# Axial attention in a two-layer encoder: products with the values issued in batches behind every fourth head

## The chip, the cores and the metric

The kernel runs on one core of a Trainium2 chip. The metric is the device time of one execution in microseconds (us). Engines: PE does matmuls and transposes, DVE element-wise work and reductions, ACT activations and copies, SP issues most of the transfers; each runs its own queue in order, and they meet in semaphores.

## The reference

Two groups of tokens, a prompt of 512 and a sample of 1024, go through the same two layers (1024 channels). The second layer's mixer is axial attention; its core is plain softmax attention within each group, in blocks of 128 queries, with 16 heads of 64 channels and 4 key/value heads:

```python
def attend(qi):
    s = jnp.einsum('bqkgd,bskd->bkgqs', qi, k).astype(jnp.float32) * scale
    p = jax.nn.softmax(s, axis=-1).astype(v.dtype)
    return jnp.einsum('bkgqs,bskd->bqkgd', p, v)
```

Everything else (projections, rotary, the first layer's convolution and window attention, a mixture of experts behind each mixer, layer norms) is the same before and after.

## The kernel before

The function axial_attention (from L1790) is one stage of the program. It runs over the prompt part (4 tiles of 128 queries against 512 keys), then the sample part (8 tiles against 1024 keys). A tile has two sides, each with a **set** of 8 heads; so the prompt part has 8 sets, the sample part 16.

For each head n of a set the chain over the engines is:

- PE, `qk` (L1884): scores of 128 queries against all keys into one of two score buffers, s_ps. Two heads share one buffer in turn, so qk waits until the exponential of the head two before has read it. The call stands two heads ahead (AHEAD = 2).
- DVE, `top` (L1938): the row maximum of s_ps. ACT, `exps` (L1981): exponential and row sum into p. DVE, `invert` (L1942): the reciprocal of the sum. ACT, `norm` (L1986): p times the reciprocal.
- PE, `turn` (L1892): transposes p block by block into t_ps (one buffer); it waits for norm of this head and for the copy of the head before. DVE, `copy` (L1949): t_ps to pT.

A set's pT is used one set later: PE, `pv` (L1899), multiplies it with the values, one key block k at a call, accumulating in o_ps. ACT, `out` (L1990), copies o_ps to cat, once in a set, behind `norm` of head 2 of a later set (behind the last set of a part, at the end).

The order on each engine is written out by hand and does not depend on time. PE, for each head n: qk(n+2), turn(n), and pv(set before, n) while n is below the number of key blocks, which is 4 in the prompt part and 8 in the sample part. DVE: top(n), copy(n-2), invert(n). ACT: exps(n), norm(n), and out behind n = 2. The first set of a part has no set before it and so no products; behind a part's last set the products of all key blocks of that set follow in a row. Middle tiles run in a hardware loop.

Of the kernel before, what the change touches and what calls it, by code (L numbers as in the profile page):

```python
# [14 lines left out]
P = 128  # L15
# [1773 lines left out]
def axial_attention(c, m, keys, values, cat, early):  # L1789
    nc = c.nc  # L1790
    SET = AX_H // 2
    SHARE = SET // 2
    AHEAD = 2
    NB = 4
    with c.stage():
        ident = c.sb("ident", [P, P])
        q = c.sb("q", [P, 2, SET * P], F32R)
        p = c.sb("p", [P, NB, SEQ[1]])
        pT = c.sb("pT", [P, 2, SEQ[1] // P, SET, P])
        col = c.sb("col", [P, NB, 4])  # L1800
        s_ps, t_ps, o_ps = [c.ps("s_ps0", SEQ[1]), c.ps("s_ps1", SEQ[1])], c.ps("t_ps", SEQ[1]), [c.ps("o_ps0", HALF), c.ps("o_ps1", HALF)]
# [12 lines left out]
        def schedule(eng, g, run):  # L1814


            first, tiles = GROUP_FIRST[g], GROUP_TILES[g]
            run(first, 0, 0, False)
            run(first, 1, 1, False)
            with eng.Fori(0, tiles - 2) as i:  # L1820
                run(i + (first + 1), 0, 2, False)
                run(i + (first + 1), 1, 2, False)
            run(first + tiles - 1, 0, 2, False)
            run(first + tiles - 1, 1, 2, True)

        def set_before(tile, side):
            return (tile, 0) if side == 1 else (tile - 1, 1)

        def number(tile, side, n=0):

            return tile * AX_H + (side * SET + n)

        with c.block() as block:

            @block.sync
            def _(sp):
                sp.dma_start(ident[:], m["ident"]).then_inc(loaded, 16)
                def load(t):
                    for side in range(2):

                        sp.wait_ge(scores, number(t, side, SET))
                        sp.dma_start(q[:, side, :].bitcast(F32), m["qT_parts"][bass.ds(t * P, P), side * SET * P:(side + 1) * SET * P]).then_inc(q_in[side], 16)

                load(0)
                for to in range(2):
                    sp.dma_start(group(to, 1, 1).bitcast(F32), group(1, 1, 0).bitcast(F32)).then_inc(spread_in, 16)
                with sp.Fori(1, GROUP_TILES[0]) as t:
                    load(t)
                sp.wait_ge(spread_in, 32)
                sp.dma_start(group(1, 1, 0).bitcast(F32), group(0, 1, 0).bitcast(F32)).then_inc(spread_in, 16)  # L1850
                with sp.Fori(GROUP_TILES[0], GROUP_TILES[0] + 2) as t:
                    load(t)

                sp.wait_ge(scores, number(GROUP_TILES[0], 0, 2 * SET))
                for k in range(len(early)):
                    for side, rows in enumerate(out_weight_rows(m, 1, k)):
                        sp.dma_start(early[k][DH * side:DH * (side + 1)], rows.rearrange("p (j n) -> p j n", j=2)).then_inc(weights_in, 16)
                with sp.Fori(GROUP_TILES[0] + 2, TILES) as t:
                    load(t)
                sp.wait_ge(weights_in, 32 * len(early))  # L1860

            @block.tensor
            def _(pe):
                pe.sem_inc(scores, 2 * SET)
                pe.sem_inc(pT_done, NB)
                pe.sem_inc(pv_done, 2)
                pe.wait_ge(loaded, 16)
                for g in range(len(SEQ)):
                    nk, first = SEQ[g], GROUP_FIRST[g]
                    if g == 0:  # L1870
                        pe.wait_ge(keys_ready, 1)
                    else:
                        pe.wait_ge(spread_in, 48)

                    def qk(tile, side, n):
                        if n >= SET:
                            tile, side, n = (tile, 1, n - SET) if side == 0 else (tile + 1, 0, n - SET)
                        if n == 0:
                            pe.wait_ge(q_in[side], tile * 16 + 16)
                        pe.wait_ge(expd, number(tile, side, n + 1))  # L1880
                        for b in range(nk // HALF):
                            at = first * P + b * HALF
                            for part in range(2):
                                last = nc.tensor.matmul(s_ps[n % 2][:, b * HALF:(b + 1) * HALF], q[:, side, n * P:(n + 1) * P],  # L1884
                                                        keys[:, part * AX_KV + 2 * side + n // SHARE, at:at + HALF], start=(part == 0), stop=(part == 1))
                        last.then_inc(scores, 1)

                    def turn(tile, side, n):
                        pe.wait_ge(p_ready, number(tile, side, n + 1))
                        pe.wait_ge(pT_ready, number(tile, side, n + 1))  # L1890
                        for k in range(nk // P):
                            last = nc.tensor.transpose(t_ps[:, k * P:(k + 1) * P], p[:, n % NB, k * P:(k + 1) * P], ident[:])  # L1892
                        last.then_inc(pT_done, 1)

                    def pv(tile, side, k):
                        if k == 0:
                            pe.wait_ge(o_out, tile * 2 + side + 1)
                        for kv in range(2):
                            last = nc.tensor.matmul(o_ps[side][DH * kv:DH * (kv + 1), :], values[:, first + k, (2 * side + kv) * DH:(2 * side + kv + 1) * DH],  # L1899
                                                    pT[:, side, k, SHARE * kv:SHARE * (kv + 1), :].rearrange("p h n -> p (h n)"),  # L1900
                                                    start=(k == 0), stop=(k == nk // P - 1))
                        if k == nk // P - 1:
                            last.then_inc(pv_done, 1)

                    def run(tile, side, before, at_last):
                        for n in range(SET):
                            if not (at_last and n + AHEAD >= SET):
                                qk(tile, side, n + AHEAD)
                            turn(tile, side, n)
                            if before and n < nk // P:  # L1910

                                pv(*set_before(tile, side), n)

                    for n in range(AHEAD):
                        qk(first, 0, n)
                    schedule(pe, g, run)
                    pe.wait_ge(pT_ready, number(first + GROUP_TILES[g], 0, 1))
                    for k in range(nk // P):
                        pv(first + GROUP_TILES[g] - 1, 1, k)

            @block.vector
            def _(v):
# [10 lines left out]
                for g in range(len(SEQ)):  # L1933
                    nk, first = SEQ[g], GROUP_FIRST[g]

                    def top(tile, side, n):
                        v.wait_ge(scores, number(tile, side, n + 1 + 2 * SET))
                        nc.vector.tensor_reduce(col[:, n % NB, 0:1], s_ps[n % 2][:, 0:nk], AX.X, ALU.max, negate=True).then_inc(top_ready, 1)  # L1938

                    def invert(tile, side, n):  # L1940
                        v.wait_ge(expd, number(tile, side, n + 3))
                        nc.vector.reciprocal(col[:, n % NB, 2:3], col[:, n % NB, 1:2]).then_inc(inverse, 1)  # L1942

# [134 lines left out]
def trunk(nc, m):  # L2078
# [6 lines left out]
    with c.stage():  # L2085
# [23 lines left out]
        with c.stage():  # L2109
            assert next_address(nc) == at_keys  # L2110
            under_keys = nc.alloc_sbuf_tensor_at("under_keys", [P, 2 * AX_KV, TOK], F32, offset=at_keys)
            keys, values = c.sb("keys", [P, 2 * AX_KV, TOK], F32R), c.sb("values", [P, TILES, AX_KVD])
            project_axial(c, m, keys, values, at_keys, under_picks, soon)
            cat = c.sb("cat", [P, KD, TOK])
            early = [early_weight(under_keys, k) for k in range(3)]
            axial_attention(c, m, keys, values, cat, early)

            project_out(c, m, 1, early, m["x2"], cat, picks, keys[:].rearrange("p k n -> p (k n)"))
# [49 lines left out]
```

## Time and profile before

| what | value |
|---|---|
| median of three runs | 3653.29 us (3652.67 to 3654.38) |
| the profiled execution's own time | 3651.85 us |
| its span | 3650.1 us |
| axial attention in it, first score product to last product with values | 1929.7 to 2449.0 us |
| PE, DVE, ACT busy over the whole span | 91%, 70%, 56% |
| PE's granted clock, mean over the span | 0.954 |

The page's shares are means over all stages; experts, projections and the first layer hold most of the span. What the change touches lies within the 519 us of axial attention: 128 us of prompt part and 393 us of sample part. So the views that count are cut to that stretch: busy time by window, and the instructions in order of time with the idle time before each and what ended it. A PE row with a count (x8) is a group of merged matmuls; its start is exact, its end is modelled, so distances between PE groups are read from start to start. In traces each matmul of the products appears as two rows, so one key block (two matmuls) is x4.

### The profile page before, as it was taken

How to read it: one execution, taken by the hardware profiler on the slowest of the kernel's cores; microseconds unless marked ns; L12 is line 12 of the kernel's file. 1: busy time of each engine (PE TensorE's matmuls, PEld its weight loads, DVE VectorE, ACT ScalarE, POOL GpSimd, SP SyncE). 2: the span in 40 equal slices, each digit the busy share in tenths (PEclk: the TensorE clock that was granted, in tenths of full speed). 3: DMA queues.
4: the chain of work that ended last, by engine and by line, in shares of the span. 5: the costliest groups of instructions: out<-in, count | busy, mean ns of one | idle time of the engine just before them, and what ended most of it. 6: DMA issues, size and time to landing. Idle time of an engine off the chain costs nothing. (4 is left out here: it accounts for less than half of the span.)

```text
span 3650.1 us, 51757 instructions
## 1 busy us (share of the span) xinstructions
PE 3305.2 (91%) x18872; PEld 2770.0 (76%) x18872; DVE 2544.8 (70%) x4025; ACT 2031.4 (56%) x2823; POOL 391.0 (11%) x309
## 2 busy tenths in 40 slices
PE   8995779599999999978987899999869999999993
PEld 7883468499999999966873456658769999999992
DVE  4988945776676766747766788875666676666765
ACT  3117942266666666643437788762246666666664
POOL 0000011111111111102210000001111111111102
PEclk9998989699999999998988999999879999999996
DMA  3001223577777777753322110013277787777864
GB/s 125 32 33 42 67 78 117 168 256 251 255 241 246 259 247 248 240 166 108 108 77 76 35 41 23 23 38 125 98 258 253 234 259 247 259 246 237 258 218 158
DMA packets 361095, 588.84 MB, mean 161 GB/s; under 512 B 17680, under 2 KB 284048, under 8 KB 359440
## 3 DMA queue, kind: packets, MB, share of 16 engines
q1 hardware_dynamic: 339728, 511.75, 41.7%
q0 software_dynamic: 14336, 50.34, 6.1%
q10 hardware_dynamic: 6912, 25.17, 1.7%
q8 instruction: 73, 1.20, 0.1%
q14 instruction: 46, 0.38, 0.0%
HBM read 505.42 MB, written 78.64 MB: 160 GB/s over the span
## 5 line engine op out<-in xcount | busy, mean ns | idle before, releaser
L1256 PE MATMUL h_ps<-xT,high 128*128 128x384 f32 x3584 | 1068.5, 360 | 2.7 <-DVE xT L1378 2.7
L1374 DVE TENSOR_TENSOR low<-raw,high 128x2048 fp32r<-128x2048 f32 x384 | 876.8, 2284 | 155.8 <-ACT high L1318 148.4
L1257 PE MATMUL h_ps<-xT,low 128*128 128x192 f32 x3584 | 906.7, 253 | 0.0
L1318 ACT ACTIVATE high<-raw 128x2048 fp32r<-128x2048 f32 x384 | 734.3, 1913 | 283.4 <-PE yp_ps L1289 176.2
L1257 PEld LDWEIGHTS h_ps<-xT,low 128*128 128x128 f32 x3584 | 686.4, 192 | 1.3
L1256 PEld LDWEIGHTS h_ps<-xT,high 128*128 128x128 f32 x3584 | 677.0, 189 | 5.0 <-issue 3.5
L1439 DVE TENSOR_TENSOR gate_up<-h_ps,cross 128x384 f32<-128x384 f32 x256 | 142.7, 558 | 298.8 <-ACT cross L1337 298.8
L1337 ACT ACTIVATE cross<-h_ps 128x384 f32<-128x384 f32 x256 | 125.6, 491 | 264.9 <-PE h_ps L1260 264.8
L200 DVE SCALAR_TENSOR_TENSOR cat<-glu,taps,cat 128x272 f32<-128x272 f32 (+33 forms) x480 | 256.7, 603 | 0.0
L1938 DVE TENSOR_REDUCE col<-s_ps 128x1 f32<-128x1024 f32 (+1 forms) x192 | 200.4, 1044 | 62.2 <-PE s_ps L1884 61.8
L1981 ACT ACTIVATE p<-s_ps,col 128x1024 f32<-128x1024 f32 (+1 forms) x192 | 186.5, 971 | 57.8 <-DVE col L1938 57.8
L1986 ACT ACTIVATE p<-p,col 128x1024 f32<-128x1024 f32 (+1 forms) x192 | 193.5, 1008 | 44.3 <-DVE col L1942 44.3
L1884 PEld LDWEIGHTS s_ps<-keys,q 128*128 128x128 f32 x640 | 106.4, 190 | 146.0 <-issue 130.9
L1884 PE MATMUL s_ps<-keys,q 128*128 128x512 f32 x640 | 199.6, 426 | 14.5 <-DMA q<-rows_qT_parts 12.0
L1280 PE MATMUL y_ps<-low,hT 128*128 128x512 f32 x512 | 204.1, 399 | 0.0
L1279 PE MATMUL y_ps<-high,hT 128*128 128x512 f32 x512 | 204.0, 398 | 0.0
L1285 PE MATMUL yp_ps<-high,hT 128*128 128x512 f32 x512 | 201.9, 394 | 0.0
L1289 PE MATMUL yp_ps<-low,hT 128*64 128x512 f32 x512 | 201.7, 394 | 0.0
L1949 DVE COPY pT<-t_ps 128x1024 f32<-128x1024 f32 (+1 forms) x192 | 198.9, 1036 | 3.4 <-PE t_ps L1892 3.4
L1278 PE MATMUL y_ps<-high,hT 128*128 128x512 f32 x512 | 201.2, 393 | 0.0
L1892 PEld LDWEIGHTS t_ps<-ident,p 128*128 128x128 f32 x1280 | 148.0, 141 | 65.6 <-ACT p L1986 26.6
L1892 PE MATMUL t_ps<-ident,p 128*128 128x128 f32 x1280 | 172.7, 274 | 26.3 <-DVE pT L1949 26.1
(254 smaller groups left out, 5943.3 us busy)
## 6 DMA issues: line engine op xcount, KB each, us to landing
raw<-moe_w_gate SPq DMA_DIRECT2D x128, 1024.0 KB, 5.3
raw<-moe_w_up SPq DMA_DIRECT2D x128, 1024.0 KB, 7.7
raw<-moe_w_down SPq DMA_DIRECT2D x128, 1024.0 KB, 7.0
rows_x<-x ACTq DMA_DIRECT2D x24, 512.0 KB, 2.6
rows_acc<-ax ACTq DMA_DIRECT2D x24, 512.0 KB, 2.7
r<-rows_acc SPq DMA_DIRECT2D x24, 512.0 KB, 5.9
rows_qT_parts<-q_turned SPq DMA_DIRECT2D x12, 1024.0 KB, 4.0
q<-rows_qT_parts SPq DMA_DIRECT2D x24, 512.0 KB, 3.8
```

The costliest lines, as they stand in the source:

```text
L200: return nc.vector.scalar_tensor_tensor(conv[:, one, lo:hi], glu[:, one, lo + step:hi + step], weight, conv[:, one, lo:hi], ALU.mult, ALU.add)
L1256: nc.tensor.matmul(ps, wh[:, n, k, :], xT[:, u, place(k), :, :].rearrange("p s n -> p (s n)"), start=(k == 0), stop=False)
L1257: nc.tensor.matmul(ps[:, 0:SLOTS], wl[:, n, k, :], xT[:, u, place(k), 0, :], start=False, stop=False)
L1278: nc.tensor.matmul(y_ps[:, cols], hT[:, f, 0:SC], wh[:, j, cols], start=first, stop=False)
L1279: nc.tensor.matmul(y_ps[:, cols], hT[:, f, SC + 2 * PC:2 * SLOTS], wh[:, j, cols], start=False, stop=False)
L1280: nc.tensor.matmul(y_ps[:, cols], hT[:, f, 0:SC], wl[:, j, cols], start=False, stop=end)
L1285: return nc.tensor.matmul(yp_ps[:, cols], hT[:, f, SC:SC + 2 * PC], wh[:, j, cols], start=first, stop=end)
L1289: return nc.tensor.matmul(yp_ps[0:PC, cols], hT[:, f, SC:SLOTS], wl[:, j, cols], start=False, stop=False)
L1318: nc.scalar.activation(split_view(high, at), piece_view(at), ACT.Copy).then_inc(high_ready, 1)
L1374: nc.vector.tensor_tensor(split_view(low, at), piece_view(at), split_view(high, at).bitcast(F32), ALU.subtract).then_inc(low_ready, 1)
L1884: last = nc.tensor.matmul(s_ps[n % 2][:, b * HALF:(b + 1) * HALF], q[:, side, n * P:(n + 1) * P], keys[:, part * AX_KV + 2 * side + n // S ...
L1892: last = nc.tensor.transpose(t_ps[:, k * P:(k + 1) * P], p[:, n % NB, k * P:(k + 1) * P], ident[:])
```

## The change

On PE alone, the call of pv moves. Where each of a set's first heads had one key block of products behind its transposes, now the heads 3 and 7 have several: in the sample part four blocks each, in the prompt part two each. The other heads have none. The order of the blocks, the buffers, the semaphores and the other engines' programs stay.

```diff
     NB = 4
+    TOGETHER = 4
...
                             turn(tile, side, n)
-                            if before and n < nk // P:
-
-                                pv(*set_before(tile, side), n)
+                            if before and n % TOGETHER == TOGETHER - 1:
+                                steps = nk // P * TOGETHER // SET
+                                for k in range(n // TOGETHER * steps, n // TOGETHER * steps + steps):
+                                    pv(*set_before(tile, side), k)
```

PE's queue in the sample part, second set, heads 0 to 3, before (s_ps are scores, t_ps transposes, o_ps products with the values; the numbers tell buffers apart):

```order
L1884 MATMUL s_ps_297<-keys,q 128x512 x4
L1892 MATMUL t_ps<-ident,p 128x128 x8
L1899 MATMUL o_ps_300<-pT,values 64x512 x2
L1884 MATMUL s_ps_298<-keys,q 128x512 x4
L1892 MATMUL t_ps<-ident,p 128x128 x8
L1899 MATMUL o_ps_300<-pT,values 64x512 x2
L1884 MATMUL s_ps_297<-keys,q 128x512 x4
L1892 MATMUL t_ps<-ident,p 128x128 x8
L1899 MATMUL o_ps_300<-pT,values 64x512 x2
L1884 MATMUL s_ps_298<-keys,q 128x512 x4
L1892 MATMUL t_ps<-ident,p 128x128 x8
L1899 MATMUL o_ps_300<-pT,values 64x512 x2
```

The same heads, and the first product of the next, in PE's queue of the changed kernel, whose lines are one further on:

```order
L1885 MATMUL s_ps_297<-keys,q 128x512 x4
L1893 MATMUL t_ps<-ident,p 128x128 x8
L1885 MATMUL s_ps_298<-keys,q 128x512 x4
L1893 MATMUL t_ps<-ident,p 128x128 x8
L1885 MATMUL s_ps_297<-keys,q 128x512 x4
L1893 MATMUL t_ps<-ident,p 128x128 x8
L1885 MATMUL s_ps_298<-keys,q 128x512 x4
L1893 MATMUL t_ps<-ident,p 128x128 x8
L1900 MATMUL o_ps_300<-pT,values 64x512 x8
L1885 MATMUL s_ps_297<-keys,q 128x512 x4
```

Four calls of one block have become one row of four blocks (eight matmuls), which stands between the transposes of head 3 and the scores of head 6.

PE's queue in the prompt part, second set, heads 4 to 7, in the changed kernel; before, these rows held s_ps and t_ps alone:

```order
L1885 MATMUL s_ps_297<-keys,q 128x512 x2
L1893 MATMUL t_ps<-ident,p 128x128 x4
L1885 MATMUL s_ps_298<-keys,q 128x512 x2
L1893 MATMUL t_ps<-ident,p 128x128 x4
L1885 MATMUL s_ps_297<-keys,q 128x512 x2
L1893 MATMUL t_ps<-ident,p 128x128 x4
L1885 MATMUL s_ps_298<-keys,q 128x512 x2
L1893 MATMUL t_ps<-ident,p 128x128 x4
L1900 MATMUL o_ps_300<-pT,values 64x512 x4
```

Two blocks that stood behind heads 2 and 3 stand behind head 7 now. DVE's queue in the sample part, which is the same before and after but for the line numbers (here before):

```order
L1938 TENSOR_REDUCE col<-s_ps_297 128x1
L1949 COPY pT<-t_ps 128x8x128
L1942 RECIPROCAL col<-col 128x1
L1938 TENSOR_REDUCE col<-s_ps_298 128x1
L1949 COPY pT<-t_ps 128x8x128
L1942 RECIPROCAL col<-col 128x1
```

Nothing moved there: maximum n, copy n-2, reciprocal n, and then the maximum of the next head.

## Rows read from the trace of the kernel before

**Rows 1.** The page's head: span and instructions of the profiled execution.
```profile
span 3650.1 us, 51757 instructions
```
**Rows 2.** Busy us (instructions) of PE, PEld, DVE, ACT, POOL by window, clock, DMA.
```profile
2056.00:2080.00 24.00, 17.71 (x98) 12.63 (x96) 19.21 (x24) 20.10 (x26) 0.00 (x0) 1.00 0.07 23
2150.00:2250.00 100.00, 100.00 (x533) 59.70 (x532) 84.03 (x101) 79.88 (x105) 0.00 (x0) 1.00 0.06 21
```
**Rows 3.** Order of time (start, duration, instruction): sample part, heads with products.
```profile
2089.91 1.08 PE L1899 MATMUL o_ps<-pT,values 128*64 128x512 f32 x4
...
2090.92 1.19 PE L1884 MATMUL s_ps<-keys,q 128*128 128x512 f32 x4
...
2091.95 1.03 PE L1892 MATMUL t_ps<-ident,p 128*128 128x128 f32 x8
2092.15 1.22 DVE L1938 TENSOR_REDUCE col<-s_ps 128x1 f32<-128x1024 f32 x1 [0.34 <-PE s_ps L1884]
...
2092.92 1.08 PE L1899 MATMUL o_ps<-pT,values 128*64 128x512 f32 x4
```
**Rows 4.** Order of time: sample part, first set, heads without products.
```profile
2065.09 1.20 DVE L1938 TENSOR_REDUCE col<-s_ps 128x1 f32<-128x1024 f32 x1
...
2066.21 1.21 DVE L1949 COPY pT<-t_ps 128x1024 f32<-128x1024 f32 x1
2066.32 1.12 ACT L1981 ACTIVATE p<-s_ps,col 128x1024 f32<-128x1024 f32 x1
...
2067.56 0.17 DVE L1942 RECIPROCAL col<-col 128x1 f32<-128x1 f32 x1
2067.57 1.06 PE L1892 MATMUL t_ps<-ident,p 128*128 128x128 f32 x8 [0.57 <-DVE pT L1949]
2067.64 1.21 DVE L1938 TENSOR_REDUCE col<-s_ps 128x1 f32<-128x1024 f32 x1
2067.76 1.15 ACT L1986 ACTIVATE p<-p,col 128x1024 f32<-128x1024 f32 x1 [0.23 <-DVE col L1942]
...
2068.39 1.17 PE L1884 MATMUL s_ps<-keys,q 128*128 128x512 f32 x4
2068.88 1.12 ACT L1981 ACTIVATE p<-s_ps,col 128x1024 f32<-128x1024 f32 x1
```
**Rows 5.** Order of time: end of the prompt part, four blocks of products in a row.
```profile
2050.96 5.27 PE L1899 MATMUL o_ps<-pT,values 128*64 128x512 f32 x16 [0.78 <-DVE pT L1949]
2051.87 0.24 PEld L1899 LDWEIGHTS o_ps<-pT,values 128*64 128x64 f32 x2 [0.61 <-issue]
2052.73 0.24 PEld L1899 LDWEIGHTS o_ps<-pT,values 128*64 128x64 f32 x2 [0.62 <-issue]
```
**Rows 6.** Order of time: ACT's evacuation of the products, sample part.
```profile
2110.92 0.58 ACT L1990 ACTIVATE cat<-o_ps 128x512 f32 x1
```
**Rows 7.** Order of time: sample part, first transposes of set 2, final eight blocks.
```profile
2082.91 1.06 PE L1892 MATMUL t_ps<-ident,p 128*128 128x128 f32 x8 [0.56 <-DVE pT L1949]
...
2441.89 7.09 PE L1899 MATMUL o_ps<-pT,values 128*64 128x512 f32 x32 [0.31 <-DVE pT L1949]
```
**Rows 8.** Order of time: prompt part, from heads without to heads with products.
```profile
1974.59 0.69 DVE L1938 TENSOR_REDUCE col<-s_ps 128x1 f32<-128x512 f32 x1
...
1976.02 0.63 PE L1892 MATMUL t_ps<-ident,p 128*128 128x128 f32 x4 [0.53 <-DVE pT L1949]
...
1976.22 0.69 DVE L1938 TENSOR_REDUCE col<-s_ps 128x1 f32<-128x512 f32 x1
...
1976.58 1.08 PE L1899 MATMUL o_ps<-pT,values 128*64 128x512 f32 x4
...
1977.59 0.73 PE L1884 MATMUL s_ps<-keys,q 128*128 128x512 f32 x2
...
1978.35 0.69 DVE L1938 TENSOR_REDUCE col<-s_ps 128x1 f32<-128x512 f32 x1 [0.43 <-PE s_ps L1884]
...
1978.68 1.08 PE L1899 MATMUL o_ps<-pT,values 128*64 128x512 f32 x4
```
**Rows 9.** Order of time: prompt part, first transposes of set 2.
```profile
1945.95 0.63 PE L1892 MATMUL t_ps<-ident,p 128*128 128x128 f32 x4 [0.54 <-DVE pT L1949]
```

## The prediction, made before the changed kernel was run

> **What bounds the kernel now.** I read the page first, then the windows of the stage, then the order of time in it, because the change touches one stage only and the page's shares mix all of them. The profiled execution spans 3650.1 us [rows 1]; its own time is 3651.85 us, 1.75 us more, and the median of three runs is 3653.29 us. So a difference read from the trace is added to 3653.29 at the end.
>
> The windows [rows 2] hold the point of departure. In the sample part, where products with the values run (the second row), PE is busy 100.00 of 100 us, DVE 84 and ACT 80. In the first set of the sample part, which has no such products (the first row), PE is busy 17.71 of 24 us and DVE and ACT 19 to 20, with little idle between their instructions. The granted clock is 1.00 in both. So there are two regimes in one stage, and the order of time shows what limits each.
>
> With the products [rows 3]: PE goes o_ps, s_ps, t_ps, o_ps without a gap, at 2089.91, 2090.92, 2091.95 and 2092.92. A head costs 1.01 + 1.03 + 0.97 = 3.01 us of PE, and the next maximum on DVE has waited 0.34 us for PE. PE is the bound.
>
> Without them [rows 4]: maximum to maximum is 2067.64 - 2065.09 = 2.55 us. The loop goes from the maximum (2065.09) to the exponential (2066.32) to the reciprocal (2067.56) to the next maximum (2067.64). PE needs only 1.03 (s_ps to t_ps, [rows 3]) + 0.82 (t_ps 2067.57 to s_ps 2068.39, [rows 4]) = 1.85 us for such a head. DVE and ACT are the bound, and ACT has no slack either: the scaling at 2067.76 is followed by the next exponential at 2068.88, as it ends.
>
> So a head's floor is 2.55 us on DVE/ACT, and the products put 3.01 - 1.85 = 1.16 us of PE into each head, spread evenly. The whole question is what happens if that work comes in lumps.
>
> **What the change does, part by part.** The same matmuls are issued (on PE in another order; on DVE and ACT every instruction stands where it stood), so no work is removed or added; no DMA and no queue of SP or POOL is moved.
>
> *Gain on PE.* Products that follow one another are cheaper than one block between other matmuls. At the end of the prompt part four blocks run in a row: the weight loads that start a new block stand at 2051.87 and 2052.73, 0.86 us apart [rows 5]; between other matmuls a block takes 1.01 us to the next s_ps [rows 3]. A lump of four costs 3 x 0.86 + 1.01 = 3.59 us in place of 4.04. Per four heads PE's work goes from 4 x 3.01 = 12.04 us to 4 x 1.85 + (0.97 + 3.59 - 0.82) = 11.14 us. If PE stayed the bound this would be the result: 0.9 us less per four heads.
>
> *Loss by coupling.* PE stands in order, and behind the lump on PE stands the score product of head n+3 (s_ps). DVE's queue is fixed: maximum n, copy n-2, reciprocal n, maximum n+1. When the lump starts behind the transposes of head 3, scores exist for heads up to 5 and no more. In the regime that DVE sets, the transposes of head 3 start 0.15 us after the copy of head 2 has ended (2066.21 + 1.21 = 2067.42 to 2067.57 [rows 4]). From that copy's end DVE has left: reciprocal 4, maximum 5, copy 3, reciprocal 5, together about 0.17 + 1.21 + 1.21 + 0.17 = 2.8 us, that is up to about 1.7 us after the lump's start. Then maximum 6 waits for s_ps of head 6, which PE starts only 3.59 us after the lump's start and which is there 1.23 us later (2090.92 to 2092.15 [rows 3]), at 4.82 us. DVE and behind it ACT stand for about 3 us in each lump. PE then waits in turn: heads 4 to 7 come from DVE and ACT again at their floor.
>
> *One round of four heads, sample part*, from the start of one lump to the start of the next: lump to s_ps 3.59; s_ps to maximum 6, 1.23; two heads at DVE/ACT's floor, maximum 6 to 8, 5.10; maximum 8 to the transposes of head 7 behind the copy of head 6, 2067.57 - 2065.09 = 2.48 [rows 4]; transposes to lump 0.97 [rows 3]. Sum 13.37 us, against 12.04 before: +1.33. The transposes of head 4 (1.03 after s_ps) and the scores of 7 and 8 come before DVE asks for them, so nothing else is late.
>
> *The evacuation.* ACT's copy of o_ps to cat takes 0.58 us once in a set, behind head 2's scaling [rows 6]. Before, ACT had waiting time there. Afterwards it falls into the heads just behind a lump, at ACT's floor, where it delays the next exponential, hence the reciprocal, hence the next maximum. I count it in full, 0.58 in every second round, and keep 0 as the other end.
>
> *Sum, sample part.* The second set's first transposes start at 2082.91 and its fourth would start three heads at 2.55 later, at 2090.56 (before: three heads at 3.01, so 1.4 us are won here). From there to the eighth head of the last set are 14 sets of 8 and 4 heads, 29 rounds, of which 14 hold an evacuation: 29 x 13.37 + 14 x 0.58 = 395.8 us. That puts the last set's eighth transposes at 2486.4; 0.97 + 4 x 0.86 = 4.4 us later the final eight blocks start, at 2490.8. Before they start at 2441.89 [rows 7]. Loss 48.9 us. The final eight blocks are the same in both.
>
> *Prompt part.* DVE's floor is 1.63 us (maximum 1974.59 to 1976.22 [rows 8]); the products come in heads 0 to 3 alone, 2.10 us a head (1976.58 to 1978.68, o_ps to o_ps). After the change two lumps of two blocks. A round: 0.86 + 1.01 to s_ps, 0.76 to the maximum (1977.59 to 1978.35), two heads 3.26, maximum to the next head's transposes 1.43 (1974.59 to 1976.02), 0.56 to the lump: 7.88 us, and 0.58 in every second one. First transposes of the second set 1945.95 [rows 9], the fourth 4.89 later at 1950.84; 13 rounds with 6 evacuations, 13 x 7.88 + 6 x 0.58 = 105.9, to 2056.8; 0.56 + 2 x 0.86 later, 2059.0, the final four blocks, before at 2050.96 [rows 5]. Loss 8.1 us.
>
> Together 48.9 + 8.1 = 57 us: 3653.3 + 57 = **3710 us**. Later stages begin later and are not touched.
>
> *Unknown sizes.* If the evacuation is hidden, 14 x 0.58 + 6 x 0.58 = 11.6 us less, 3698. If a block in a lump costs 1.01 and not 0.86, 29 x 0.45 + 13 x 0.15 = 15 us more, 3725. I take the rows' middle course, evacuation in full (nearest row: ACT back to back in rows 4) and 0.86 (nearest row: the same four blocks in a row).
>
> **The rivals.**
> *The lump is hidden and only the PE gain is left (faster).* This needs DVE and ACT to have enough queued at a lump's start to work until s_ps returns, 4.82 us of it where I count about 1.7. It breaks even when the standing time of 3 us shrinks to about 1.4. Then a round costs PE's 11.14 us, 0.9 less than now, 29 times, and in the prompt part DVE's floor, 4 x 1.63 = 6.5 in place of 2 x (2.10 + 1.63) = 7.5, 13 times: 26 + 13 = 39 us, 3614 us. For it: PE is busy 100% in the row where the products run, and blocks in a row are cheaper. Against it: two banks of scores, so only two heads ahead, and DVE's fixed order. 5%.
>
> The Trainium skill speaks for this rival: Perfetto Trace Analysis, Matmul Optimizations, says that the matmul engine scales its power with its use and that matmuls should therefore run back to back in batches. The trace gives that no room by way of the clock, since 1.00 is granted in both windows [rows 2]; by the rule with the cheaper blocks alone the time would be this rival's 3614 us, by the rows with the coupling 3710 us.
>
> *Partly hidden, gain and stall cancel.* A stall of about 1.4 us in a round; nothing in the rows sets it so. Within 0.2% (about what a measurement of this kernel can tell from no change), near 3653. 2%.
>
> *The lump is wholly in series.* If maximum 5 and copy 3 gain nothing beside the lump, a round is four heads at 2.55 and the lump's 3.74, 13.94 in place of 13.37: 29 x 0.57 = 17 us more, 3727, and with dearer blocks up to 3742. Against it: the scores of head 5 stand in PE's queue before the lump. 8%.
>
> **How the numbers follow.** The forecast, 3710 us with 3694 to 3728 about it, has 85%: 3698 and 3725 are its computed ends, and some 4 us are added for what rows of one execution leave open. The range is that one; what is left out is the two small cases on the fast side and the upper part of the serial one. Faster by over 0.2% 5%, within 2%, slower 93%.
>
> **What would show it.** In the profile after: rounds in the sample part of about 13.4 and 13.9 us, o_ps in rows of four blocks 3.6 us from the next s_ps; idle time of DVE before its maximum of about 3 us, twice in a set; PE waiting about 0.6 us for pT in the heads without products; PE near 83% (11.14 of 13.37) in windows where it had 100%; the stage longer by 57 us and the rest as before. Wrong would be: PE without gaps in the sample part (the first rival), no long waits of the maximum for s_ps, or a granted clock other than 1.00 there, since all durations are from rows at that clock.

## The result, and the profile after

The changed kernel takes 3715.19 us (median of four runs, 3712.45 to 3716.38) against 3653.81 us of the kernel before in the same comparison: 61.4 us more, a ratio of 1.0166 with a 95% interval of 1.0151 to 1.0181. The forecast was 3710 us, 57 us more, in a range of 3694 to 3728.

The page of the changed kernel begins like this (span, then busy time of each engine, its share and its instructions):

```profile
span 3714.6 us, 51757 instructions
PE 3295.9 (89%) x18872; PEld 2771.6 (75%) x18872; DVE 2538.8 (68%) x4025; ACT 2029.1 (55%) x2823; POOL 384.4 (10%) x309
```

The number of instructions is that of [rows 1], and PE's busy time is a little less (3305.2 us before): no work was added, so the time is waiting. Axial attention runs from its first score product to its last product with the values for 520.2 us before (its first score product starts at 1928.7 us, not at 1929.7) and 582.1 us after, 61.9 us more, so the difference lies there; the whole span is 64.5 us longer, of which 3.1 us had come before the stage began.

The window of the sample part after the change (us of PE, PEld, DVE, ACT, POOL; then granted clock and transfers), which answers to the second row of [rows 2]:

```profile
2103.00:2486.00 383.00, 322.48 (x1784) 199.77 (x1780) 275.00 (x335) 267.08 (x349) 0.00 (x0) 1.00 0.07 22
```

PE is busy 84% where it was busy 100%, DVE 72% where it was 84%. The clock is 1.00 as before. All engines are less busy: they wait for one another.

PE in order of time, one round of the sample part (start, duration, instruction, idle time before and what ended it), which answers to the PE rows of [rows 3]:

```profile
2197.81 1.07 PE L1893 MATMUL t_ps<-ident,p 128*128 128x128 f32 x8 [0.60 <-DVE pT L1951]
2198.80 3.65 PE L1900 MATMUL o_ps<-pT,values 128*64 128x512 f32 x16
2202.39 1.21 PE L1885 MATMUL s_ps<-keys,q 128*128 128x512 f32 x4
2203.43 1.04 PE L1893 MATMUL t_ps<-ident,p 128*128 128x128 f32 x8
2204.22 1.17 PE L1885 MATMUL s_ps<-keys,q 128*128 128x512 f32 x4
...
2212.68 3.65 PE L1900 MATMUL o_ps<-pT,values 128*64 128x512 f32 x16
```

There are four blocks in one lump, 3.59 us to the next scores, and 13.88 us from lump to lump. This is a round with an evacuation (ACT's copy of o_ps to cat); a round without one takes 13.50 us. DVE in the same stretch:

```profile
2199.04 1.22 DVE L1951 COPY pT<-t_ps 128x1024 f32<-128x1024 f32 x1
2200.39 0.17 DVE L1944 RECIPROCAL col<-col 128x1 f32<-128x1 f32 x1
2203.63 1.22 DVE L1940 TENSOR_REDUCE col<-s_ps 128x1 f32<-128x1024 f32 x1 [3.07 <-PE s_ps L1885]
2204.77 1.21 DVE L1951 COPY pT<-t_ps 128x1024 f32<-128x1024 f32 x1
```

DVE has finished its last reciprocal 1.76 us after the lump's start (2200.56) and stands until the scores are there, 4.83 us after it. The idle time before the maximum is 3.07 us, where [rows 3] had 0.34. The totals of waiting over 300 us of the sample part (us in total, times, longest):

```profile
DVE col L1940 <- PE s_ps L1885: 64.4, 21, 3.1
PE t_ps L1893 <- DVE pT L1951: 48.4, 66, 1.0
```

The waits go both ways. DVE waits once in a round, about 3.07 us; PE then waits in each of the other three heads, 0.73 us on average, for DVE's copy to free t_ps. Before, in the same stretch of time, DVE's waits were 34.2 us in 100 small ones, and PE's waits of this kind came to 1.1 us in all the sample part's heads with products but the last two (2080 to 2436 us).

### The profile page after: what moved, and what is told of

It is laid out like the page before. It is cut to its first block and busy times, and to the rows that moved or that the text cites. A ratio compares the mean times of both kernels' runs of the same rounds, so it can differ in the third digit from the quotient of the medians.

```text
span 3714.6 us, 51757 instructions
## 1 busy us (share of the span) xinstructions
PE 3295.9 (89%) x18872; PEld 2771.6 (75%) x18872; DVE 2538.8 (68%) x4025; ACT 2029.1 (55%) x2823; POOL 384.4 (10%) x309
## 5 line engine op out<-in xcount | busy, mean ns | idle before, releaser
L1184 POOL TENSOR_TENSOR still<-still 128x1 f32<-128x1 f32 x98 | 26.1, 268 | 1609.2 <-DVE work L1456 1297.3
```

## The experiments

The first theory is that of the prediction: a lump on PE holds back the scores and the transposes that DVE needs, DVE and ACT run dry, and PE then waits for them in turn. Its rivals: PE stays the bound and gains by cheaper blocks; the lump stands wholly in series; the two score buffers alone are the reason. In every run below only axial attention differs from one of the two kernels.

| run | us | ratio to before, 95% |
|---|---|---|
| e1, lumps in the sample part only | 3706.6 | 1.0146 (1.0129 to 1.0163) |
| e2, lumps in the prompt part only | 3661.6 | 1.0020 (1.0011 to 1.0030) |
| e3, lumps half as large | 3686.1 | 1.0086 (1.0069 to 1.0103) |
| e5, scores ahead of the lump | 3693.8 | 1.0105 (1.0088 to 1.0122) |
| e6, evacuation one head earlier | 3707.6 | 1.0149 (1.0134 to 1.0165) |
| e7, prompt part in half blocks | 3662.6 | 1.0024 (1.0014 to 1.0034) |
| e8, two transpose buffers, every second head | 3640.6 | 0.9966 (0.9952 to 0.9979) |
| e9, two transpose buffers alone | 3649.8 | 0.9990 (0.9980 to 0.9999) |
| e10, lumps with two transpose buffers | 3651.4 | 0.9997 (0.9988 to 1.0006) |

### e1 and e2: each part by itself

The condition at the call of pv is made to depend on the part g (0 the prompt, 1 the sample); e2 has `g == 0`:

```diff
+                            if g == 1:
+                                if before and n % TOGETHER == TOGETHER - 1:
+                                    steps = nk // P * TOGETHER // SET
+                                    for k in range(n // TOGETHER * steps, n // TOGETHER * steps + steps):
+                                        pv(*set_before(tile, side), k)
+                            elif before and n < nk // P:
+                                pv(*set_before(tile, side), n)
```

> Lumps of four blocks in the sample part only; the prompt part as in the kernel before. Theory (PE's lump holds back the next scores and transposes, DVE and ACT stand for about 3 us, every round goes from 12.04 to about 13.4 and 13.9 us): the sample part's whole loss, 49 us by the forecast's sum and about 54 by the changed kernel's trace, so 3703 to 3708 us; the prompt part's sets stay near 15.05 us. Rival (the parts act on each other, say by the granted clock or the transfers): less than 45 us or more than 60 us.

> Lumps of two blocks in the prompt part only; the sample part as in the kernel before. Theory: 8 us over the kernel before, 3662 us, with prompt rounds of 7.9 and 8.4 us in place of 7.5, and the sample part's sets at 24.05 us. Rival (in the prompt part DVE's floor alone counts, since PE has room): about 13 us faster than before, 3641 us.

Measured: 3706.6 us, 53 us more than before (3653.9), and 3661.6 us, 8 us more. Together 61 us, what the whole change costs. The sets of the part left alone are unchanged (3.00 to 3.01 us a head in the sample part of e2). The two parts add up and do not act on each other; the rivals of both are out.

### e3: lumps half as large

```diff
-    TOGETHER = 4
+    TOGETHER = 2
```

> Lumps of two blocks behind every second head in the sample part, one block behind every second head in the prompt part. Theory: a round of two heads in the sample part is lump to scores 0.86 + 1.01, scores to maximum 1.23, maximum to the next head's transposes 2.48, transposes to lump 0.97, together 6.55 us in place of 6.02; 59 rounds, 31 us; the evacuation falls into DVE's and ACT's standing time and costs nothing; the prompt part's round is 1.01 + 0.76 + 1.43 + 0.56 = 3.76 us, as much as two heads now on average. So about 3685 us, half the change's loss with half its lump. Rival one (PE stays the bound and gains by blocks in a row): 5.72 us a round, 17 us faster, 3637. Rival two (the lump is in series with DVE's floor): 7.1 us a round, 64 us slower, 3718.

Measured: 3686.1 us, 32 us more than before. In the sample part every round is 6.59 or 6.60 us (6.55 expected), in the prompt part 3.77 (3.76). DVE and PE in order of time, sample part of e3:

```profile
2193.06 1.94 PE L1900 MATMUL o_ps<-pT,values 128*64 128x512 f32 x8
2194.93 1.20 PE L1885 MATMUL s_ps<-keys,q 128*128 128x512 f32 x4
...
2196.16 1.23 DVE L1940 TENSOR_REDUCE col<-s_ps 128x1 f32<-128x1024 f32 x1 [0.98 <-PE s_ps L1885]
...
2198.67 1.06 PE L1893 MATMUL t_ps<-ident,p 128*128 128x128 f32 x8 [0.74 <-DVE pT L1951]
```

The lump is 1.87 us to the next scores instead of 3.59. The cheaper-blocks rival (3637) and the serial one (3718) are both out, on opposite sides. In the sample part, where all of this loss lies, it grows with the lump, but not in proportion: that part is 34 us longer than before with lumps of two blocks and 54 us with lumps of four. The prompt part of e3, with one block behind every second head, is 2 us shorter than before in the trace.

### e5: the scores ahead of the lump

```diff
-                            if not (at_last and n + AHEAD >= SET):
+                            early = n == TOGETHER if before else False
+                            early = early or (n == 0 and before == 2)
+                            if not early and not (at_last and n + AHEAD >= SET):
                                 qk(tile, side, n + AHEAD)
                             turn(tile, side, n)
+                            if before and n % TOGETHER == TOGETHER - 1 and not (at_last and n + AHEAD + 1 >= SET):
+                                qk(tile, side, n + AHEAD + 1)
```

> The changed kernel with one move on PE: the scores of head n+3 are issued ahead of the lump and not behind it, in both parts. The third score product finds its buffer free, since the exponential of the head two before is over by then. Theory (both products of PE that DVE needs, scores and transposes, stand behind the lump): the wait only moves from the maximum of head 6 to the copy of head 4, a round in the sample part falls from 13.4 to about 12.9 us and in the prompt part from 7.9 to 7.65: 14 and 3 us less than the changed kernel, 3698 us. Rival (the two score buffers alone are the reason): with the scores there in time the stall is gone and PE's 11.1 us a round remain, 3614 us. Rival (place of the scores is no matter): 3715 us.

Measured: 3693.8 us, 21 us less than the changed kernel and still 40 us more than before. The rounds of the sample part are 12.95 us, 13.22 to 13.25 where the hardware loop turns and 13.42 with an evacuation. DVE and PE in order of time:

```profile
2201.51 3.65 PE L1900 MATMUL o_ps<-pT,values 128*64 128x512 f32 x16
2202.17 0.16 DVE L1948 RECIPROCAL col<-col 128x1 f32<-128x1 f32 x1
2202.27 1.22 DVE L1944 TENSOR_REDUCE col<-s_ps 128x1 f32<-128x1024 f32 x1
2205.09 1.09 PE L1893 MATMUL t_ps<-ident,p 128*128 128x128 f32 x8
2206.22 1.22 DVE L1955 COPY pT<-t_ps 128x1024 f32<-128x1024 f32 x1 [2.73 <-PE t_ps L1893]
```

The maximum runs beside the lump now, and then DVE stands 2.73 us before the next copy, which waits for the transposes behind the lump. The wait has moved, as expected, so the score buffers are not the reason by themselves: DVE needs two products of PE for each head, and both stand behind the lump. The gain was 21 us and not 17: in the trace the sample part gave 15 us (14 expected) and the prompt part 6 (3 expected; its plain rounds are 7.43 us and not 7.65).

### e6: the evacuation one head earlier

```diff
-                            if n == AHEAD and before == 2:
+                            if n == 1 and before == 2:
```

> The changed kernel with ACT's evacuation of o_ps one head earlier, behind head 1's scaling and not head 2's. There ACT stands idle in the lump behind head 7. Theory: the evacuation then costs nothing; by the forecast's sum 20 x 0.58 = 11.6 us less than the changed kernel, by the rounds of its trace (13.88 with it, 13.50 without; 8.36 and 7.92 in the prompt part) 14 x 0.38 + 6 x 0.44 = 8 us less: 3704 to 3707 us. Rival (it was hidden already and the longer rounds come from elsewhere): 3715 us.

Measured: 3707.6 us, 7.6 us less than the changed kernel's 3715.2. ACT and DVE in order of time, sample part of e6:

```profile
2197.38 0.60 ACT L1992 ACTIVATE cat<-o_ps 128x512 f32 x1 [0.85 <-PE o_ps L1900]
2198.41 1.23 DVE L1940 TENSOR_REDUCE col<-s_ps 128x1 f32<-128x1024 f32 x1 [3.06 <-PE s_ps L1885]
2199.67 1.11 ACT L1983 ACTIVATE p<-s_ps,col 128x1024 f32<-128x1024 f32 x1 [1.69 <-DVE col L1940]
```

The copy of 0.60 us lies in time in which ACT waits anyway, and the rounds of 13.88 us are gone: three of four are 13.50 to 13.52, and the fourth, where the loop turns, 13.80 to 13.82. So the evacuation did cost something in the changed kernel, 0.37 us a set in the sample part and not 0.58.

### e7: the prompt part in half blocks

The change's opposite, on the kernel before: half a key block behind each head of the prompt part.

```diff
-                            if before and n < nk // P:
-
+                            if before and g == 0:
+                                pv(*set_before(tile, side), n // 2, (n % 2,))
+                            elif before:
                                 pv(*set_before(tile, side), n)
```

Here pv takes the list of its matmuls as an argument, and waits and signals only at the first and last of the set.

> The kernel before with the change's opposite in the prompt part: each of the 8 heads of a set has half a key block of products (one of its two matmuls), where heads 0 to 3 had one block each; the sample part as before. Theory (PE's work should be spread as evenly as DVE's floor allows): a head costs PE 0.53 + 0.58 + 0.57 = 1.68 us, near DVE's 1.63, so a set takes 13.4 us in place of 15.05: 7 sets, 11 us faster than before, 3643 us. Rival (two half blocks apart lose what runs side by side in one block, so that half a block costs as much as a whole one): 2.1 us a head, 16.8 a set, 12 us slower, 3666 us.

Measured: 3662.6 us, 9 us slower than before. The price that the theory put on half a block was wrong here, and the rival held (3666 by its sum). PE in order of time, prompt part of e7:

```profile
1955.35 1.07 PE L1899 MATMUL o_ps<-pT,values 128*64 128x512 f32 x2
1956.35 0.73 PE L1884 MATMUL s_ps<-keys,q 128*128 128x512 f32 x2
1956.92 0.60 PE L1892 MATMUL t_ps<-ident,p 128*128 128x128 f32 x4
1957.45 1.07 PE L1899 MATMUL o_ps<-pT,values 128*64 128x512 f32 x2
```

One matmul (x2 in the trace) takes 1.00 us to the next scores, and [rows 8] have 1.01 us for the two of a whole block (x4). The two write different halves of o_ps's partitions and run side by side: in the trace of the kernel before their rows start within 0.01 us of each other. Taken apart, each costs as much as both. Each head takes 2.10 us, all eight of a set.

### e8, e9 and e10: room for PE to run ahead

In the prompt part a head's transposes fill half of t_ps. With the two halves used in turn the transposes wait for the copy of the head two before. e9 has this alone:

```diff
-                        pe.wait_ge(pT_ready, number(tile, side, n + 1))
+                        pe.wait_ge(pT_ready, number(tile, side, n + 1 + g))
+                        at = 0 if g else (n % 2) * HALF
...
-                v.sem_inc(pT_ready, 1)
+                v.sem_inc(pT_ready, 2)
```

Transposes and copy use columns from `at` on. In e9 the first products of a set also wait for the last copy of that set, since the transposes no longer do. e10 has the two halves and the lumps of e2; e8 has the two halves and one block behind every second head, by this edit:

```diff
-                            if before and n < nk // P:
-
-                                pv(*set_before(tile, side), n)
+                            if before and (g or n % 2):
+                                pv(*set_before(tile, side), n if g else n // 2)
```

> The kernel before with two edits in the prompt part, nothing in the sample part: the transposes go to two halves of t_ps in turn, so that they wait for the copy of the head two before and not of the head before; and one block of products stands behind every second head, where it stood behind heads 0 to 3. Theory (PE's work must come evenly, and PE must be allowed to run ahead of DVE): two heads need 2 x 1.1 + 1.0 = 3.2 us of PE and 3.26 of DVE and ACT, so a set takes about 13.3 us in place of 15.05: 12 us faster than before, 3641 us. Rival (the transposes' one buffer was no matter): rounds of 3.77 us as with products behind every second head and one buffer, no change, 3654 us.

> The control for the run before: two halves of t_ps in the prompt part alone, the products where they were, behind heads 0 to 3. Theory: four heads in a row still need 2.1 us of PE each, and two score buffers let PE run ahead by part of a head only, so 0 to 1 us a set, 0 to 7 us faster, about 3650 us. Rival (the buffer does it all): 12 us faster, 3641 us.

> Lumps of two blocks in the prompt part only, as in the run with the prompt part alone, and two halves of t_ps in turn there. Theory (a lump costs what PE cannot have done ahead): PE reaches the lump earlier, the lump's scores still come behind it, so the wait of the maximum shrinks but stays, a round of 7.9 us becomes about 7.4: 6 us less than 3661.6, 3655 us. Rival (the score buffers alone count): 3661.6. Rival (the lump is hidden with one buffer more): DVE's floor, 6.5 us a round, 3642 us.

Measured: e8 3640.6 us, 13 us faster than before and the best version here; e9 3649.8, 4 us faster, and its heads with products still take 2.10 us each; e10 3651.4, 10 us less than the same lumps with one buffer (e2; 6 were expected) and not to be told from the kernel before. PE and DVE in order of time, prompt part of e8:

```profile
1997.91 1.08 PE L1900 MATMUL o_ps<-pT,values 128*64 128x512 f32 x4
...
1998.08 0.69 DVE L1938 TENSOR_REDUCE col<-s_ps 128x1 f32<-128x512 f32 x1
1998.92 0.73 PE L1884 MATMUL s_ps<-keys,q 128*128 128x512 f32 x2
...
1999.71 0.69 DVE L1938 TENSOR_REDUCE col<-s_ps 128x1 f32<-128x512 f32 x1
...
2001.18 1.08 PE L1900 MATMUL o_ps<-pT,values 128*64 128x512 f32 x4
```

Two heads take 3.24 to 3.27 us, 3.73 with an evacuation (3.77 in e3, with the same order of products and one buffer), DVE does not wait for the scores, and DVE's floor of 1.63 us is nearly reached. DVE's waiting in e10, behind a lump:

```profile
1982.13 0.69 DVE L1944 TENSOR_REDUCE col<-s_ps 128x1 f32<-128x512 f32 x1 [0.77 <-PE s_ps L1885]
```

With one buffer it was 1.30 us in the changed kernel's prompt part; the rounds fall from 7.9 and 8.37 to 7.37 and 7.84. So what a lump costs depends on how far PE could work ahead of it: with more room the same lump costs less, and with more room and single blocks DVE does not wait for PE at all. The sample part was not tried in this way: there a head's transposes fill all of t_ps.

## Why the prediction was right

**The bound and the regimes.** Right. PE without gaps became PE with a gap in three of four heads (0.56 to 0.97 us), all but the one right behind a lump, and DVE's and ACT's floor sets those heads.

**The coupling.** Right, to 0.1 us. The forecast had DVE done about 1.7 us after the lump's start (1.76 measured), the scores at 4.82 (4.83) and 3 us of standing (3.07). e5 showed that the scores are only the first of two products that come late; the sum for its rounds, with the transposes of head 4 behind the lump too, came within 0.05 us of the shorter ones (12.9 and 12.95).

**The block at 0.86 us.** The value was right, its reading was not. In [rows 5] I took the weight loads at 2051.87 and 2052.73 for the starts of two blocks. A block has four such rows, so those two (x2 each) start half blocks, at the lower of the clock's two levels (1.2 and 2.4 GHz). The window around them, before the change, shows it:

```profile
2051.00:2053.00 2.00, 2.00 (x6) 0.73 (x8) 0.00 (x0) 0.00 (x0) 0.00 (x0) 0.50 0.00 0
```

The granted clock is 0.50 there, the lower level; it is 1.00 in the lumps of the sample part. At the upper level half blocks are 0.43 us apart, in the lump of the changed kernel:

```profile
2199.28 0.14 PEld L1900 LDWEIGHTS o_ps<-pT,values 128*64 128x64 f32 x2 [0.29 <-issue]
2199.71 0.14 PEld L1900 LDWEIGHTS o_ps<-pT,values 128*64 128x64 f32 x2 [0.28 <-issue]
2200.14 0.14 PEld L1900 LDWEIGHTS o_ps<-pT,values 128*64 128x64 f32 x2 [0.29 <-issue]
```

Twice 0.43 is 0.86, so the two errors, half a block taken for a block and the lower clock for the upper, cancelled: that the term came out right is luck. The sample part's last row of [rows 7], eight blocks in 7.09 us, would have given it soundly.

**The rounds.** 28 of them lie between the first lump (2102.75) and the last (2487.59) of the sample part, 384.8 us; the forecast's terms give 28 x 13.37 + 14 x 0.58 = 382.5, 2.4 us less (384.84 and 382.48). The rounds are 13.50 where nothing is added, 13.88 with an evacuation, and 13.80 to 13.83 where the hardware loop turns, once in a tile, with idle time of DVE ahead of a maximum that no engine ended:

```profile
2222.99 1.23 DVE L1940 TENSOR_REDUCE col<-s_ps 128x1 f32<-128x1024 f32 x1 [0.24 <-issue]
```

So the evacuation was sized too high (0.37 to 0.38 for 0.58), the plain round too low by 0.13, and the loop's turn was left out. Of the 0.13 us, 0.08 is the floor of a head, which stands twice in a round: maxima are 2.59 us apart in the rounds, where [rows 4] had 2.55. The evacuation's error and the others partly cancel.

**The end of the sample part.** Left out: here the granted clock falls. The last transposes of the changed kernel:

```profile
2494.91 1.06 PE L1893 MATMUL t_ps<-ident,p 128*128 128x128 f32 x8 [0.74 <-DVE pT L1951]
2497.47 1.92 PE L1893 MATMUL t_ps<-ident,p 128*128 128x128 f32 x8 [1.49 <-DVE pT L1951]
2500.80 1.94 PE L1893 MATMUL t_ps<-ident,p 128*128 128x128 f32 x8 [1.41 <-DVE pT L1951]
2502.67 11.32 PE L1900 MATMUL o_ps<-pT,values 128*64 128x512 f32 x48
```

In the last two heads there are neither scores nor products left, PE waits 1.4 to 1.5 us for DVE twice, and the eight transposes take 1.92 us where they took 1.06. From the last lump's place at a plain round (2487.59 + 13.37) to the final 12 blocks it is 1.7 us more, and these take 0.8 us more than the same 12 blocks in e6, whose clock did not fall. Before, one block stood behind each of these heads, and the window from 2436 to 2442 had a clock of 1.00. That 2.5 us and the rounds' 2.4 make 4.9 of the 5.0 us by which the sample part's loss, 53.9 us in the trace, exceeds the forecast's 48.9. The same place in e6, with the same products and the same waits:

```profile
2488.12 1.06 PE L1893 MATMUL t_ps<-ident,p 128*128 128x128 f32 x8 [1.49 <-DVE pT L1951]
2490.60 1.06 PE L1893 MATMUL t_ps<-ident,p 128*128 128x128 f32 x8 [1.41 <-DVE pT L1951]
2491.59 10.52 PE L1900 MATMUL o_ps<-pT,values 128*64 128x512 f32 x48
```

The granted clock is 1.00 here. In e1 it fell between these two heads (transposes of 1.06 and then 1.94 us behind the same waits). So the waits by themselves do not decide it. What does is open, and it is open too how many executions of the changed kernel pay these 2.5 us.

**The prompt part.** 8.0 us in the trace, 8.1 forecast; 8 us in e2 by itself. DVE's wait behind a lump is 1.30 us. The agreement is in part luck, since errors of the sample part's kinds cancel: plain rounds are 7.84 to 7.99 us (7.88 forecast), rounds with an evacuation 8.33 to 8.37 (8.46), and the one in which the loop turns is 8.34.

**The rivals.** The faster one did not come: PE is not the bound behind a lump. The cheaper blocks that it counts on are there, 0.45 us a lump (3.59 for 4.04), and the rounds are 1.5 to 1.9 us longer all the same. The rule that goes with this rival, in the Trainium skill (Perfetto Trace Analysis, Matmul Optimizations), gives the engine's power, which follows its use, as the reason for batches; no run here shows a gain of that kind, since the clock is 1.00 in the sample part before and in the rounds after. In e8 the products stand one by one, not in batches, and that is the fastest version measured. The serial rival is out by e3.

## What to carry to other kernels

On an engine that works in order, work without an urgent reader should go in pieces no larger than the slack that its urgent readers have; what one gains by batching is to be set against what the others have queued when the batch starts. Write the queue of the waiting engine down, up to the first instruction that needs something from behind the batch: here that gave the stall to a tenth of a microsecond. If the stall is to go, look at every product that the waiting engine needs and not at the first one late, and try a second buffer for the busy engine together with a better order. In the prompt part the order alone (e3) left the rounds as long as before, the buffer alone (e9) gave 4 us, and both (e8) gave 13.

## What the runs showed of the hardware

- Two fp32 matmuls of 64 output columns, whose results go to the two halves of o_ps's partitions, take as long together as one of them alone: 1.01 us in [rows 8], 1.00 us for one in e7.
- In the last two heads of the sample part PE has only transposes to do, with waits of 1.4 to 1.5 us before them. The granted clock fell to the lower level there in the traces of the changed kernel (transposes from 1.06 to 1.92 us, a window's mean of 0.81), of e1 and of e5, and stayed at 1.00 in that of e6 with the same waits as in the changed kernel. It stayed at 1.00 in rounds in which PE waits 0.6 to 1.0 us in three of four heads and is busy 84%. The row of the changed kernel's window:

```profile
2490.00:2502.00 12.00, 8.36 (x44) 6.04 (x41) 6.16 (x7) 5.17 (x7) 0.00 (x0) 0.81 0.00 0
```
